# Hybrid attention encoder on one core: value blocks loaded and awaited by half, keys loaded by high and low part

## The reference

```python
C_PATTERNS = ((128, 1), (512, 4), (2048, 16))        # (window, dilation) of its three groups
for g, (w, d) in enumerate(C_PATTERNS):
    off = jnp.arange(-(w // (2 * d)), w // (2 * d) + 1) * d
    idx = qpos[:, None] + off[None, :]
    s = einsum(q[:, :, g], k_g[:, idx]) + bias_g      # masked where idx is outside
    lse = logsumexp(s); o = einsum(exp(s - lse), v_g[:, idx])
alpha = softmax(stack(lse))                           # over the three groups
y = sum(o_g * alpha_g)
```

## Time and profile before

| | |
|---|---|
| three runs, median (lowest to highest) | 2765.29 us (2764.78 to 2768.25) |
| the profiled execution | 2772.11 us, span 2769.8 us |
| busy: TensorE / its weight loads | 99% / 88% |
| busy: VectorE, ScalarE, GpSimd | 58%, 43%, 28% |
| HBM read and written | 159 GB/s over the span |
| one layer's quads (24 steps) | 55 us (layer 0), 59 us (layer 1) |

### The profile page before, as it was taken

How to read it: one execution, slowest core, us unless ns; L and a number is a source line. 1 busy time by engine, 2 the same in 40 slices (tenths; PEclk the granted TensorE clock), 3 DMA queues, 4 the chain that set the end, 5 groups by cost and what they waited for, 6 DMA issues and landing times. The chain is left out here.

```text
span 2769.8 us, 43315 instructions
## 1 busy us (share of the span) xinstructions
PE 2732.1 (99%) x14505; PEld 2447.6 (88%) x14505; DVE 1609.7 (58%) x3865; ACT 1184.4 (43%) x2813; POOL 763.8 (28%) x882
## 2 busy tenths in 40 slices
PE   8999999999999999999999999999999999999999
PEld 7888899988999999988888888999889999999887
DVE  3345644434676677677743465444346767776776
ACT  4322222224565566544542222222246655665443
POOL 0333333320343344300003334333203433443000
PEclk9999999999999999999999999999999999999999
DMA  5356566668544542464524565656774445325535
GB/s 175 106 183 200 180 185 188 181 179 233 142 132 123 128 112 82 177 219 130 197 85 142 176 195 173 200 170 188 191 218 134 117 118 149 101 69 217 192 122 182
DMA packets 436214, 442.52 MB, mean 160 GB/s; under 512 B 97591, under 2 KB 327127, under 8 KB 435996
## 3 DMA queue, kind: packets, MB, share of 16 engines
q1 hardware_dynamic: 435996, 439.77, 53.3%
HBM read 313.91 MB, written 125.75 MB: 159 GB/s over the span
## 5 line engine op out<-in xcount | busy, mean ns | idle before, releaser
L1834 ACT CAST w_hi<-w_raw 128x512 fp32r<-128x512 f32 x640 | 397.0, 622 | 697.8 <-PE bank L1605 430.6
L1603 PE MATMUL bank<-w_hi,act_hi 128*128 128x512 f32 x1728 | 689.2, 399 | 0.0
L2120 DVE TENSOR_TENSOR w_lo<-w_raw,w_hi 128x512 fp32r<-128x512 f32 x640 | 460.1, 722 | 384.9 <-ACT w_hi L1834 383.3
L1605 PE MATMUL bank<-w_hi,act_lo 128*128 128x512 f32 x1728 | 679.0, 393 | 0.0
L1604 PE MATMUL bank<-w_lo,act_hi 128*128 128x512 f32 x1728 | 677.6, 392 | 0.0
L1605 PEld LDWEIGHTS bank<-w_hi,act_lo 128*128 128x128 f32 x1728 | 372.6, 216 | 54.1
L1603 PEld LDWEIGHTS bank<-w_hi,act_hi 128*128 128x128 f32 x1728 | 373.3, 216 | 50.1
L1604 PEld LDWEIGHTS bank<-w_lo,act_hi 128*128 128x128 f32 x1728 | 373.3, 216 | 48.7
L1659 PE MATMUL bank<-act_hi,w_hi 128*128 128x384 f32 x1024 | 349.2, 341 | 0.0
L1661 PE MATMUL bank<-act_hi,w_lo 128*128 128x384 f32 x1024 | 346.3, 338 | 0.0
L1660 PE MATMUL bank<-act_lo,w_hi 128*128 128x384 f32 x1024 | 345.7, 338 | 0.0
(11 more groups left out here) (136 smaller groups left out, 4406.5 us busy)
## 6 DMA issues: line engine op xcount, KB each, us to landing
w_raw<-w_in SPq DMA_DIRECT2D x144, 512.0 KB, 4.8
w_sums<-sum_out SPq DMA_DIRECT2D x32, 1280.0 KB, 6.7
w_raw<-w_sums SPq DMA_DIRECT2D x80, 512.0 KB, 4.0
sum_in<-w_out SPq DMA_DIRECT2D x64, 512.0 KB, 5.6
heads_t<-turned SPq DMA_DIRECT2D x240, 128.0 KB, 2.4
q_t<-heads_t SPq DMA_DIRECT2D x192, 128.0 KB, 2.1
k_t<-keys_t SPq DMA_DIRECT2D x48, 384.0 KB, 5.8
w_raw<-w_out SPq DMA_DIRECT2D x32, 512.0 KB, 3.7
```

The costliest lines, as they stand in the source:

```text
L1603: pe.matmul(acc[t][:], hi, w_hi[:, W_AT[n]:W_AT[n] + SLAB], start=(k == 0), stop=False)
L1605: last = pe.matmul(acc[t][:], lo, w_hi[:, W_AT[n]:W_AT[n] + SLAB], start=False, stop=(k == KC - 1))
L1834: nc.scalar.copy(w_hi[:, W_AT[n]:W_AT[n] + SLAB], w_raw[:, load % W_RAW, j, :]).then_inc(w_hi_done, 1)
L2120: nc.vector.tensor_tensor(w_lo[:, W_AT[n]:W_AT[n] + SLAB], w_raw[:, load % W_RAW, j, :], w_hi[:, W_AT[n]:W_AT[n] + SLAB].bitcast(F32), ALU ...
```

## The change

Three things. Unit 3's blocks are loaded half by half: half 0, class by class, once the packed unit before has used half 0 for its last time (its third product) instead of the unit's last one, then half 1. Each half has a semaphore, and TensorE waits for the half it reads. A load of keys still has two DMAs, but one now carries the high part to all 128 partitions and the other the low part, where before one carried both parts to partitions 0 to 63 and the other to 64 to 127; the source is a pattern written by hand whose outermost dimension, of 2 entries and step 0, reads the head's 64 rows twice.

By `at_items`, unit 3's eight block loads stand at items 17, 18, 19, 20 (half 0) and 20, 21, 22, 23 (half 1), ahead of the bias pieces of the same item.

```diff
@@ -634,8 +634,8 @@
-BLOCKS_AT = at_items(((u, c), UNIT_LAST[u - KV_SLOTS] + PAIR_LAG + c)
-                     for u, x in enumerate(ATT_UNITS) if packed(x) and u >= KV_SLOTS for c in range(CLASSES))
+BLOCKS_AT = at_items(((u, half, c), UNIT_START[u - KV_SLOTS] + (half + 1) * (TT // 2) - 1 + PAIR_LAG + c)
+                     for u, x in enumerate(ATT_UNITS) if packed(x) and u >= KV_SLOTS for half in range(2) for c in range(CLASSES))
@@ -904,7 +904,7 @@
-        blocks_loaded = sem("blocks_loaded")
+        blocks_loaded = [sem(f"blocks_loaded{i}") for i in range(2)]
@@ -1241,8 +1241,9 @@
-                for to in range(2):
-                    sp.dma_start(k_t[to * DH:(to + 1) * DH, :, slot, :, :].bitcast(F32), keys_t[unit["k"]])                        .then_inc(k_loaded[slot], 16)
+                for part in range(2):
+                    rows = bass.AP(keys_t.tensor, (unit["k"] * DH * 2 + part) * TOKENS, [[0, 2], [2 * TOKENS, DH], [1, TOKENS]])
+                    sp.dma_start(k_t[:, part, slot, :, :].rearrange("p t c -> p (t c)").bitcast(F32), rows).then_inc(k_loaded[slot], 16)
@@ -1266,16 +1267,15 @@
-            def load_blocks(l, u, c):
+            def load_blocks(l, u, half, c):
...
                 if u >= KV_SLOTS:
-                    sp.wait_ge(pv_done, l * N_STEPS + UNIT_LAST[u - KV_SLOTS] + 1)
+                    sp.wait_ge(pv_done, l * N_STEPS + UNIT_START[u - KV_SLOTS] + (half + 1) * (TT // 2))
...
-                for half in range(2):
-                    sp.dma_start(blocks[half][c * PACK:(c + 1) * PACK, :, c, 0:DH], rows[half, c]).then_inc(blocks_loaded, 16)
+                sp.dma_start(blocks[half][c * PACK:(c + 1) * PACK, :, c, 0:DH], rows[half, c]).then_inc(blocks_loaded[half], 16)
@@ -1470,8 +1470,8 @@
-                        for c in range(CLASSES):
-                            load_blocks(l, 1, c)
+                        for half, c in itertools.product(range(2), range(CLASSES)):
+                            load_blocks(l, 1, half, c)
@@ -1484,8 +1484,8 @@
-                    for u, c in BLOCKS_AT.get(it, ()):
-                        load_blocks(l, u, c)
+                    for u, half, c in BLOCKS_AT.get(it, ()):
+                        load_blocks(l, u, half, c)
@@ -1726,8 +1726,8 @@
-                    pe.wait_ge(blocks_loaded, 16 * 2 * CLASSES * (l * KV_C + st["unit"]["j"] + 1))
                     half, at = divmod(st["t"], TT // 2)
+                    pe.wait_ge(blocks_loaded[half], 16 * CLASSES * (l * KV_C + st["unit"]["j"] + 1))
```

## The result

The changed kernel takes 2920.7 us (median of 4 runs, 2916.6 to 2923.5) against 2765.0: a ratio of 1.0558, 95% interval 1.0543 to 1.0573. It is 156 us slower. The prediction was slower, 2860, with a range of 2805 to 2950. The profiled execution took 2923.5 us, span 2921.5.

What follows compares the result with a forecast made beforehand. TensorE, busy 99% of the span, was taken as the bound, with nearly all to win or lose in the quads. Keys' delays of 42.5 us plus 5 us for the clock per layer, 95 us in all, gave 2860 us; range 2805 to 2950.

Steps and rivals of the forecast that it cites:

- The hint it rested on: In the trace before, loads whose outermost count 16 does not divide lacked landing times, suggesting two engines for the keys.
- what units 5 to 11 cost: Behind the quads: queries have 24 us against 22 needed, so costed at 0; bound above 70 us.
- A unit's keys at 17 us: Keys loads: one unit's pair on two engines takes 17 us, between 15.4 and 20.2, against 5.8 before.
- Layer start: Keys of units 0 and 1 delay the value stores, so VectorE's first minima start at 668.5: plus 16 us.
- Units 2, 3 and 4: In the quads: stretches of 23, 24 and 24 us behind slow keys, adding 11, 9 and 6.5 us.
- The quads in all: Both layers' quads: 42.5 us of delays and 5 us for the clock per layer, 95 us in total.
- the clock's share: After stalls in the quads the granted clock falls: 5 us more per layer, about 1.3 us per long stall.
- the 22 that I had worked out: Behind the quads: time in us a query load needs behind slow keys, 17 + 1.5 + 1.5 + 2.
- The prediction's opening: Almost all that can be won or lost lies in the quads; behind them TensorE is busy 575 of 579 us.
- Rival A: Two engines, but queries behind units 5 to 11 also late: 40 to 90 us more, 2900 to 2950; chance 0.14.
- Part (1): Earlier block loads for unit 3 in the quads end the block wait: 5 to 10 us off over both layers.
- the part's store: In the quads, once blocks are early, this store holds step 22's minima and so step 24: gain 2.6 to 3.5 us.

Runs made afterwards that it cites:

- Units 0 and 1 alone: The changed kernel with the new keys loads only for units 0 and 1, the other units loading keys as before: 2795.7 us, ratio 1.0114.
- Units 0 to 4 alone: The changed kernel with the new keys loads only for units 0 to 4, the later units loading keys as before: 2863.7 us, ratio 1.0363.
- units 5 to 11 alone: The changed kernel with the new keys loads only for units 5 to 11, the earlier units loading keys as before: 2816.6 us, ratio 1.0184.

## Why the prediction was right, and by how much it missed

The direction and the mechanism held: the keys' source starts with a dimension of 2 and two engines carry the load, as the share of 0.13 shows. The hint it rested on, loads of 33 and 36 rows without a landing time, is now a series: 16 and 128 show one, 8, 4 and 2 do not. The Trainium skill's rule (DMA: Bandwidth & Descriptors, section Rules for kernel authors) that a leading zero-stride broadcast of c copies confines a DMA to at most c engines agrees with the series. The run with 128 different rows shows that the zero step is not needed for it; the Trainium skill says so too (the same page, section Why a DMA increments its semaphore by 16 and not by 1): the slowest dimension counts.

One step failed: what units 5 to 11 cost. It was put at 0 and is 54 us, nearly all of the 61 us between 2860 and 2921. Step by step:
- A unit's keys at 17 us, with 2 to land: queries issued just behind landed 19.2 us after the keys' issue. Right.
- Layer start, plus 16 us, first minima near 668: they start at 665.63 in place of 652.08, so 13.5 later, and unit 1's first scores at 680.29 in place of 661.85, 18.4 later, with the steps between at the lower clock. Units 0 and 1 alone cost 33 us in two layers, 2 x 16 = 32 forecast.
- Units 2, 3 and 4, forecast 23, 24 and 24 us for their stretches: steps 6, 12, 18 and 24 are scored at 680.29, 704.42, 731.69 and 757.1, so 24.1, 27.3 and 25.4.
- The quads in all: 2 x 47.5 = 95 us forecast with the clock's share. Units 0 to 4 alone take 98 us more than the kernel before, 101 more than the blocks' part alone. That it is so near is in part luck: I counted four stalls and 5 us a layer for the clock, while the quads of layer 0 ran at 0.57 in the mean and those of layer 1 (2101 to 2211) at 0.71. The steps between the layer's start and unit 1 took 4.9 us more, for which the sum had no term. What the clock alone cost is not isolated.
- Units 5 to 11, forecast 0: 54 us. First, the lead of a query load was misread. The window 706 to 1285 was taken for the 192 steps behind the quads, 3.0 us each, but it also holds 130 us of the output projection, whose first block product is at 1155.7. In the kernel before:

```profile
L1636 PE MATMUL bank<-w_hi,a_part x672: 389/389/504, 1155.7 to 2764.0; 128*128 128x512 f32 x168
```

  The steps take (1155.7 - 706.3)/192 = 2.34 us, so a query load has 18.7 us of lead where I had put 24, against the 22 that I had worked out. The 3.3 us between them, times 14 loads, are 46. That this lies near 54 is luck, for the loss is made otherwise: with units 5 to 11 alone the waits on queries are 17.3 us, in 10 waits of 3.7 at most. An estimate that fits them takes 15.1 us for a unit's keys, from the 52 GB/s of the trace, and not 17: 20.1 against 18.7, times 14, is 20. The rest had no term in the sum: the wait of all parts' stores ahead of `mixed_t` (line 2291), 15.7 us of TensorE's time in the two layers; waits on `prob_t` and `mixed_t`, 6.1 and 4.7 us more than with the blocks' part alone; and 12 us of longer busy time (2739.6 against 2727.3) at a lower granted clock (0.989 against 0.997). Together these terms are 56 us; the two profiled spans differ by 55 (2815.5 against 2760.8). The prediction's opening, that almost all that can be won or lost at once lies in the quads, was wrong for the same reason: a stretch in which TensorE is 99% busy has nothing to win, but it took a third of the loss.
- Rival A (queries late behind units 5 to 11, 2900 to 2950, chance 0.14) is what happened, in its time and in part in its mechanism. It was given its small chance by the same misread 24 us. Of its reasons, slower engines did not come true (26 GB/s for each engine behind unit 6's keys, not 19.5); SP held up did (6.83 us for the two bias loads behind unit 6's keys).
- Part (1): the block wait went, as forecast, at 3.6 us and not 8. I named the part's store as next and priced it; the item's own queries are next, in the same chain of SP. (Its reading that all other waits of TensorE are 1.5 us and less passes over one of 6.9 us for `ln_rows` at the kernel's start; nothing rests on it.)
- The Trainium skill's rule of SBUF's ports (SBUF — State Buffer, section Door 1: The DMA port swizzle), for which before showed nothing: the loads to 128 partitions land in 4.4 us with 128 different rows, in 4.7 with the keys stored twice and in 5.5 with outermost 16, against 5.8 for the pairs of 64. So the form may bring something, 0.3 to 1.4 us per load, but these runs differ in their rows too, and none of it was on the path: 2759.7 and 2762.4 have overlapping intervals.

## What to carry to other kernels

Before a DMA's access pattern is rewritten, look at the outermost count of the source as well as that of the destination: in these runs the source's count, and not the 128 partitions written, decided how many engines carried the load, and with one queue the loads issued later waited behind those engines. A load can be slow without any wait naming it; look at the landing of what is issued just behind. And cut windows at the marks of the stretch (its first and last instruction), not at round numbers, before dividing by a count of steps.

## What the runs showed of the hardware

- The number of engines follows the source's outermost dimension down to 2, whether rows repeat or not: the DMA share is 0.13 (2 of 16) with 2 and 0.25 (4 of 16) with 4, at about 26 GB/s per engine, and the times are 2760, 2761, 2776, 2805 and 2921 us for 128, 16, 8, 4 and 2. With 8 the share could not be read apart from other loads.
- The loss is not in proportion: twice the share per engine cost 16, then 45, then 161 us. Only with 2 do the queries behind units 5 to 11 come late.
- A slow load holds up the issuing queue too: SP took 6.15 us to issue one load of queries behind the keys.
- With TensorE short of work through the quads (75.5 of 107 us busy), its granted clock averaged 0.57 over 107 us; products of line 1689 that take 276 ns in the median in the kernel before took 415.
